# Six pairs of weight sums moved from the hidden loop to the gates' stage, in an fp32 encoder block on one core

## The reference

```python
h = rms(x, g_mix); z = h @ w_in
za, zu, zv, zq, zg = split(z)
ya = gelu(s5(za)); ya = (ya * sigmoid(ya @ w_glu + b_glu)) @ w_a_out
yb = sgu(zu, zv) @ w_b_out
yc = mem_xattn(zq, mem) @ w_c_out        # k, v from rms(mem, g_mem) @ w_kv
g = sigmoid(zg + b_gate)                 # three gates of width 1024
x = x + (g0 * ya + g1 * yb + g2 * yc) @ w_out
hf = rms(x, g_ffn)
x = x + (silu(hf @ w_gate) * (hf @ w_up)) @ w_down      # hidden width 2816
out = rms(x, g_final)
```

## Time and profile before

| what | value |
|---|---|
| median of three runs | 777.63 us |
| the profiled execution, its own time | 777.84 us |
| its span, first to last instruction | 776.1 us |
| TensorE busy | 765.6 us |
| VectorE busy | 541.6 us |
| ScalarE busy | 354.3 us |
| GpSimd busy | 315.8 us |
| DMA | 121.98 MB, 157 GB/s over the span |
| VectorE's sums (mix) | 44 operations, 47.2 us |

### The profile page before, as it was taken

The page is one execution under the profiler, slowest core; times in us unless marked ns, Lnnn a source line. Parts: engine busy times, 40 slices in busy tenths (PEclk is TensorE's granted clock), DMA queues, the critical chain, the costliest instruction groups (busy, mean ns, idle before and its releaser), DMA issues.

```text
span 776.1 us, 9751 instructions
## 1 busy us (share of the span) xinstructions
PE 765.6 (99%) x3576; PEld 630.8 (81%) x3576; DVE 541.6 (70%) x729; ACT 354.3 (46%) x526; POOL 315.8 (41%) x169
## 2 busy tenths in 40 slices
PE   9999999999999999999999999999999999999996
PEld 7778887788888888888888888888888888778885
DVE  6999997684848484345865677777776777635686
ACT  6896567644545434543433333332323233444463
POOL 4456646233333333444444344534444453920000
PEclk9999999999999999999999999999999999999999
DMA  7744332132222432232324465666756557677852
GB/s 274 297 142 135 110 109 86 31 102 82 82 82 82 132 139 82 82 108 84 106 96 146 147 206 180 214 230 203 228 186 196 204 200 246 196 246 249 280 179 109
DMA packets 39667, 121.98 MB, mean 157 GB/s; under 512 B 4048, under 2 KB 4176, under 8 KB 37840
## 3 DMA queue, kind: packets, MB, share of 16 engines
q1 hardware_dynamic: 39488, 121.26, 47.1%
q10 hardware_dynamic: 144, 0.26, 0.1%
HBM read 104.99 MB, written 16.52 MB: 157 GB/s over the span
## 4 chain that ended last, share of the span: by engine, by line
PE 78%; DVE 13%; ACT 3%; issue 2%; DMA 2%; POOL 1%; SPq 0%; POOLq 0%; DVEq 0%; ACTq 0%
PE bank L1557 21%; PE bank L1558 21%; PE bank L1559 21%; PE bank L1926 4%; PE bank L1928 4%; PE bank L1927 4%; DVE pow_tmp L969 3%; DVE tab_tmp L969 1%; DVE s5p L969 1%; PE bank L1798 1%; DMA xT<-xt_dram 1%; DMA raw<-mix_dram 1%; DVE m_lo L974 1%; ACT prob L655 1%; DVE h_lo L974 0%
## 5 line engine op out<-in xcount | busy, mean ns | idle before, releaser
L500 POOL TENSOR_TENSOR w_lo<-raw,w_hi 128x1024 fp32r<-128x1024 f32 x90 | 219.1, 2434 | 298.1 <-ACT w_hi L561 298.1
L561 ACT ACTIVATE w_hi<-raw 128x1024 fp32r<-128x1024 f32 x112 | 118.6, 1060 | 309.1 <-PE bank L1559 302.3
L1557 PE MATMUL bank<-h_hi,w_hi 128*128 128x512 f32 x608 | 238.2, 392 | 0.5 <-DVE th L969 0.4
L1559 PE MATMUL bank<-h_hi,w_lo 128*128 128x512 f32 x608 | 236.7, 389 | 0.0
L1558 PE MATMUL bank<-h_lo,w_hi 128*128 128x512 f32 x608 | 236.6, 389 | 0.0
L1557 PEld LDWEIGHTS bank<-h_hi,w_hi 128*128 128x128 f32 x608 | 114.1, 188 | 25.5 <-DVE th L969 1.3
L1559 PEld LDWEIGHTS bank<-h_hi,w_lo 128*128 128x128 f32 x608 | 114.1, 188 | 23.9
L1558 PEld LDWEIGHTS bank<-h_lo,w_hi 128*128 128x128 f32 x608 | 114.2, 188 | 23.3 <-issue 0.2
L505 POOL TENSOR_TENSOR w_lo<-raw,w_hi 128x512 fp32r<-128x512 f32 x48 | 67.2, 1422 | 56.3 <-ACT w_hi L561 49.7
L969 DVE TENSOR_TENSOR mix<-mix 128x512 f32<-128x512 f32 x44 | 47.2, 1072 | 10.5 <-DMA mix<-w_dram 9.4
L969 DVE TENSOR_TENSOR lo<-raw,hi 128x1536 fp32r<-128x1536 f32 (+1 forms) x19 | 33.3, 1757 | 28.8 <-ACT hi L888 28.8
(11 more groups left out here) (297 smaller groups left out, 1391.7 us busy)
## 6 DMA issues: line engine op xcount, KB each, us to landing
raw<-w_dram SPq DMA_DIRECT2D x112, 512.0 KB, 3.4
mix<-w_dram SPq DMA_DIRECT2D x11, 1024.0 KB, 7.7
mix_dram<-mix SPq DMA_DIRECT2D x11, 1024.0 KB, 6.4
raw<-w_dram SPq DMA_DIRECT2D x32, 256.0 KB, 3.9
raw<-mix_dram SPq DMA_DIRECT2D x28, 256.0 KB, 3.9
half_dram<-odd SPq DMA_DIRECT2D x11, 256.0 KB, 7.9
second<-half_dram SPq DMA_DIRECT2D x3, 768.0 KB, 6.0
raw<-mix_dram SPq DMA_DIRECT2D x3, 768.0 KB, 4.3
```

The source lines that it names most:

```text
L500: nc.gpsimd.tensor_tensor(w_lo[:, s, :], raw[:, s, :], fv(w_hi[:, s, :]), ALU.subtract).then_inc(w_ready, 1)
L561: nc.scalar.activation(w_hi[:, slot, :], raw[:, slot, :], ACT.Copy).then_inc(w_rounded, 1)
L1557: mm(out, a[0], b[0], start=first, stop=False)
L1559: return mm(out, a[1], b[0], start=False, stop=last)
```

## The change

It sets AHEAD = 6. The first six pairs are loaded, summed and stored in the stage T_J2 through three buffers: mix, mix_b (where uc was) and mix_c (where u was). SP issues these loads and stores between the weight tiles (`mix_ahead`), VectorE forms the sums between the gates (`mixed_ahead`). In the hidden loop turns 0 to 4 handle pairs 6 to 10, and turns 5 to 10 have no sums. The units get seven raw places, with a third raw_d and raw_e in the upper half of mix, and their loads another order. Three smaller edits: on VectorE the memory's `token_scale` moves ahead of the first S5 products; on ScalarE `round_weights(T_VU + 6)` moves ahead of `softmax_scale(2)`; on TensorE gate 0 of T_J1 waits for three sgu_taken, and the fourth is waited for before gate 1 of the first round.

```diff
@@ -54,6 +54,7 @@
 NS = 2
+AHEAD = 6
@@ -129,9 +130,10 @@
         raw_c = at("raw_c", o_s + (4 * C_BRE + 63) // 64 * 64, [P, TILE])
-        raw_d = [at(f"raw_d{i}", o_h + 12288 + 4096 * i, [P, TILE]) for i in range(2)]
-        unit_raw = [raw[:, 0, :], raw[:, 1, :], raw_c[:, :], raw_d[0][:, :], raw_d[1][:, :]]
-        UNIT_SLOT = (0, 1, 2, 3, 4, 0, 1, 2, 0, 1, 2)
+        raw_d = [at(f"raw_d{i}", o_h + 12288 + 4096 * i, [P, TILE]) for i in range(3)]
+        raw_e = at("raw_e", o_e + 12288, [P, TILE])
+        unit_raw = [raw[:, 0, :], raw[:, 1, :], raw_c[:, :], *(r[:, :] for r in raw_d), raw_e[:, :]]
+        UNIT_SLOT = (0, 1, 2, 3, 4, 5, 6, 0, 1, 2, 6)
         UNIT_DVE = (6, 8)
@@ -196,6 +198,7 @@
         mix = at("mix", o_e + 8192, [P, 4, WB])
+        mix_ring = [mix, at("mix_b", o_uc, [P, 4, WB]), at("mix_c", o_u, [P, 4, WB])]
         zg = at("zg", o_e, [P, 4, T])
@@ -282,7 +285,8 @@
         mix_loaded, mixed, mix_stored, half_stored = sems("mix_loaded mixed mix_stored half_stored")
-        unit_loaded = [sem(f"unit_loaded{i}") for i in range(5)]
+        unit_loaded = [sem(f"unit_loaded{i}") for i in range(7)]
+        ring_loaded = [mix_loaded, xtok_loaded[0], xtok_loaded[1]]
         unit_half, unit_dve, p5_done, s1_ready, s5_ready = sems("unit_half unit_dve p5_done s1_ready s5_ready")
@@ -382,37 +386,57 @@
             sp.dma_start(sgu[:, :, :], sgu_d).then_inc(sgu_loaded, 16)
+            def load_mix(n, buf, done=mix_loaded):
+                t = T_DN + 2 * n
+                sp.dma_start(buf[:, :, :].rearrange("p (a b) n -> p a (b n)", a=2),
+                             w_d[t:t + 2, :, :].rearrange("a p n -> p a n")).then_inc(done, 16)
+            def keep_mix(n, buf):
+                sp.wait_ge(mixed, 4 * (n + 1))
+                sp.dma_start(mix_d[n, :, :], buf[:, :, :].rearrange("p a n -> p (a n)")).then_inc(mix_stored, 16)
+            def mix_ahead(t):
+                n, odd_tile = divmod(t - T_J2 - 2, 2)
+                if odd_tile or n < 0:
+                    return
+                if n < AHEAD:
+                    if n == 0:
+                        sp.wait_ge(st_ready, ROUNDS)
+                    elif n < 3:
+                        sp.wait_ge(y_done, ROUNDS)
+                    else:
+                        sp.wait_ge(mix_stored, 16 * (n - 2))
+                    load_mix(n, mix_ring[n % 3], ring_loaded[n % 3])
+                if 2 <= n < AHEAD + 2:
+                    keep_mix(n - 2, mix_ring[(n - 2) % 3])
             for t in range(8, T_WO):
                 next_weights(t)
+                mix_ahead(t)
                 if t == T_J2 - 2:
...
                         load_x(i)
-            def load_pair(i):
-                t = T_DN + 2 * i
-                sp.dma_start(mix[:, :, :].rearrange("p (a b) n -> p a (b n)", a=2),
-                             w_d[t:t + 2, :, :].rearrange("a p n -> p a n")).then_inc(mix_loaded, 16)
-            def store_mix(i):
-                sp.wait_ge(mixed, 4 * (i + 1))
-                sp.dma_start(mix_d[i, :, :], mix[:, :, :].rearrange("p a n -> p (a n)")).then_inc(mix_stored, 16)
             def store_half(i):
...
                 next_weights(t)
+                mix_ahead(t)
                 i, j = divmod(t - T_FF, 4)
...
                     sp.wait_ge(x1_ready, 5)
-                    load_pair(0)
-                if i > 0 and j == 2:
-                    store_mix(i - 1)
+                    sp.wait_ge(mix_stored, 16 * AHEAD)
+                    load_mix(AHEAD, mix)
+                if 0 < i <= PAIRS - AHEAD and j == 2:
+                    keep_mix(AHEAD + i - 1, mix)
+                if 0 < i < PAIRS - AHEAD and j == 3:
+                    sp.wait_ge(mix_stored, 16 * (AHEAD + i))
+                    load_mix(AHEAD + i, mix)
                 if i > 0 and j == 3:
-                    sp.wait_ge(mix_stored, 16 * i)
-                    load_pair(i)
                     store_half(i - 1)
@@ -426,10 +450,12 @@
                     sp.wait_ge(w_ready, T_DN - 1 + k)
-                elif 3 <= k < 5:
+                elif 3 <= k < 6:
                     sp.wait_ge(w_used, T_DN)
-                elif k >= 5:
-                    unit_split(sp, {5: 0, 6: 1, 7: 2, 8: 5, 9: 6, 10: 7}[k])
+                elif k == 6:
+                    sp.wait_ge(mix_stored, 16 * PAIRS)
+                elif k > 6:
+                    unit_split(sp, {7: 0, 8: 1, 9: 2, 10: 6}[k])
                 sp.wait_ge(mix_stored, 16 * (k + 1))
@@ -460,14 +486,12 @@
                 load_unit(k)
-            store_mix(PAIRS - 1)
             for k in range(3, 6):
...
             store_half(PAIRS - 1)
-            for k in range(6, 10):
+            for k in range(6, PAIRS):
                 load_unit(k)
             load_three(0)
-            load_unit(10)
             load_three(1)
@@ -691,9 +715,9 @@
             round_weights(T_VU + 5)
+            round_weights(T_VU + 6)
             softmax_scale(2)
             gelu_u(1)
-            round_weights(T_VU + 6)
             round_weights(T_VU + 7)
@@ -882,7 +906,7 @@
                 if u == 0:
-                    act.wait_ge(w_ready, T_DN + 5)
+                    act.wait_ge(w_ready, T_DN + 6)
                 if u >= 2:
@@ -1097,6 +1121,8 @@
+            token_scale(2, 2, mtstd[:, :], mtrstd[:, :], mdiag[:, :, :], diag_m)
             bre, bim, cre, cim = (grid(c0) for c0 in (C_BRE, C_BIM, C_CRE, C_CIM))
@@ -1109,8 +1135,6 @@
             link(tt(bpow[1][:, L - 1, :, :], bb_tmp[:, 2, :, :], bb_tmp[:, 3, :, :], ALU.add))
-            token_scale(2, 2, mtstd[:, :], mtrstd[:, :], mdiag[:, :, :], diag_m)
             def times(to, of, a_re, a_im, conj, n):
@@ -1364,13 +1388,29 @@
+            def mix_sums(buf, count):
+                b11, b12, b21, b22 = (buf[:, j, :] for j in range(4))
+                tt(b22, b22, b12, ALU.subtract).then_inc(mixed, 1)
+                dve.wait_ge(mixed, count + 1)
+                tt(b12, b12, b11, ALU.subtract).then_inc(mixed, 1)
+                dve.wait_ge(mixed, count + 2)
+                tt(b11, b22, b11, ALU.add).then_inc(mixed, 1)
+                dve.wait_ge(mixed, count + 3)
+                tt(b21, b21, b11, ALU.subtract).then_inc(mixed, 1)
+            def mixed_ahead(n):
+                dve.wait_ge(ring_loaded[n % 3], 16 * (n // 3 + (1 if n % 3 == 0 else 2)))
+                mix_sums(mix_ring[n % 3], 4 * n)
             scale_gate0(0)
             scale_gate0(1)
+            mixed_ahead(0)
             for c in range(KB):
...
             scale_gate0(3)
+            mixed_ahead(1)
             for t in range(2):
@@ -1383,6 +1423,8 @@
             dve.wait_ge(y2_lo_s, KB)
+            mixed_ahead(2)
+            mixed_ahead(3)
             for g in (0, 2, 4, 6):
@@ -1392,7 +1434,11 @@
                     scale_gate0(g + 4)
+                    if g == 2:
+                        mixed_ahead(4)
                     scale_gate0(g + 5)
+                    if g == 2:
+                        mixed_ahead(5)
@@ -1418,21 +1464,16 @@
             a22, a12 = odd[:, 0:HALF], odd[:, HALF:T]
-            b11, b12, b21, b22 = (mix[:, j, :] for j in range(4))
-            with nc.vector.Fori(0, PAIRS) as i:
+            def hidden_pair(i, sums):
                 for n in range(2):
...
-                dve.wait_ge(mix_loaded, 16 * i + 16)
-                tt(b22, b22, b12, ALU.subtract).then_inc(mixed, 1)
-                dve.wait_ge(mixed, 4 * i + 1)
-                tt(b12, b12, b11, ALU.subtract).then_inc(mixed, 1)
-                dve.wait_ge(mixed, 4 * i + 2)
-                tt(b11, b22, b11, ALU.add).then_inc(mixed, 1)
-                dve.wait_ge(mixed, 4 * i + 3)
-                tt(b21, b21, b11, ALU.subtract).then_inc(mixed, 1)
+                if sums:
+                    dve.wait_ge(mix_loaded, 16 * i + 16 * ((AHEAD + 2) // 3 + 1))
+                    mix_sums(mix, 4 * i + 4 * AHEAD)
                 for n, hidden in enumerate((even, odd[:, :])):
@@ -1454,6 +1495,11 @@
                    ).then_inc(ff_lo, 1)
+            with nc.vector.Fori(0, PAIRS - AHEAD) as i:
+                hidden_pair(i, True)
+            with nc.vector.Fori(PAIRS - AHEAD, PAIRS) as i:
+                hidden_pair(i, False)
@@ -1757,7 +1803,7 @@
-            pe.wait_ge(sgu_taken, 4)
+            pe.wait_ge(sgu_taken, 3)
             pe.wait_ge(pt_act, 4)
@@ -1805,6 +1851,8 @@
                         pe.wait_ge(j1_g, free)
+                    elif b == 1:
+                        pe.wait_ge(sgu_taken, 4)
                     tile_ready(t0 + j)
```

## The result

The changed kernel took 784.16 us (median of four runs, 783.30 to 784.99), the kernel before beside it 777.62 (777.53 to 778.03). The ratio is 1.0082, 95% interval 1.0071 to 1.0094: slower by 6.5 us. I had forecast slower, but by 2, and the range ended at 782.0. The profiled execution took 784.99 us, with a span of 783.3.

The account below looks back on a forecast made before the run. TensorE's queue of matmuls sets the end, with at most some 10 us to win; -0.5 + 2.7 - 0.6 + 1.8 - 1.5 = +1.9 gave 779.7 against 777.84, 779.5 against the median. Range 775.2 to 782.0.

Parts of the forecast that it names:

- (1): Memory's row scale moves ahead of the tables on VectorE, removing TensorE's 0.42 us wait at 47.38: -0.5 us.
- (2): ScalarE rounds tile T_VU+6 ahead of the softmax scaling; holds by GpSimd make vM late for values(0): +2.7 us.
- rival D: Late tiles from traffic of (4), or a lower clock after TensorE's long stop: +1 to +3 on the forecast, chance 0.10.
- (3): Gate matmul waits for three sgu_taken, not four, removing the 0.43 us idle at 142.59: -0.6 us.
- (4): Six pairs' sums move from the hidden loop to the gates' stage; the last two groups delay merge0(4): +1.8 us.
- (5): Seven raw places in the down projection remove TensorE's waits before units 9 and 10: -1.5 us.

Follow-up runs that it names:

- e1: The changed kernel with the rounding of tile T_VU+6 put back behind softmax_scale(2) and gelu_u(1), nothing else; 778.46 us, ratio to before 1.0003.
- e4: As e1, with AHEAD = 4, so groups 4 and 5 are summed in the hidden loop again; 775.53 us, ratio to before 0.9971.
- e2: The changed kernel with 14 products of no use ahead of TensorE's wait for vM; 779.91 us, ratio to before 1.0024.
- e3: The kernel before with only the rounding of tile T_VU+6 moved ahead of softmax_scale(2); 781.39 us, ratio to before 1.0046.
- e7: As e1, with AHEAD = 2, so only groups 0 and 1 stay in the gates' stage; 775.05 us, ratio to before 0.9961.
- e5: As e1, but SP issues a group's store behind the odd tile, not right behind the load; 777.43 us, ratio to before 0.9993.
- e10: As e7, with the five raw places for units of before and their order of loads; 776.77 us, ratio to before 0.9988.
- e6: As e1, with the 24 sums in the gates' stage replaced by 24 small memsets, all loads and stores kept; 776.31 us, executions 774.69 to 778.07.
- e8: As e7, with the rounding of T_VU+6 between softmax_scale(2) and gelu_u(1), and vM ahead of the table sums; 777.12 us, ratio to before 0.9992.
- e9: As e8, with vM between head 3's last maximum and its snm, and head 3's reciprocal between the table sums; 773.80 us, ratio to before 0.9950.

## Why the prediction was wrong

Its steps, one by one, against the lateness in the traces:

| part | predicted | measured in the changed kernel | in other runs |
|---|---|---|---|
| (1) row scale | -0.5 | wait gone, 0 net at 118.85 | -0.4 to -0.5 (e1, e4) |
| (2) wait for vM | +2.7 | +2.5 | +2.5 (e2, e3) |
| (2) clock behind it | 0 (rival D: +2.3) | +3.0 | +1.8 (e3), 0 (e2) |
| (3) three sgu_taken | -0.6 | -0.7 | -0.7 (e1, e7); e3 has it without the edit |
| (4) gates' stage | +1.8 | +4.1 | +3.8 (e1), +2.3 (e2, e5), +0.6 (four groups), 0 (two) |
| (5) seven places | -1.5 | -1.8 | -1.8 (e1, e7), +0.5 with five (e10) |

**What held.** The chain of holds in (2) came out step by step: snm released at 128.67 for 128.8 predicted, vM at 132.25 for 132.4, values(0) at 132.30 for 132.5. That included its weakest link, that GpSimd would reach T_J1 0.2 us ahead of snm; it was 0.33. The prediction names only operations with two operands in SBUF as held, but snm has one (128x2, with a constant), and it took 2.09 us where the first snm took 0.17. In (4) without late tiles the trace of e5 also follows the working: merge0(4) 1.1 late for 1.3 predicted, a first wait of 0.40 in T_WO for 0.4, and 1.32 for mg_lo, where 379.8 to 381.7 less that 0.4 left 1.5. The waits are 1.72 of the 2.3; the rest are slow first products behind them, which I had left out. (5) was short by the slow products behind its two stops. (1) holds in e1 and e4: the lateness falls by 0.58 at the row scale, and 0.2 of it goes again at 61.94. In the changed kernel's profile ScalarE stood 1.00 us for memf at 28.70, and a wait of 0.40 for a w_lo at 36.19 took the gain back. e1 has the same list there and no such wait, so I count it to the execution.

**What failed** is one decision, twice: the two costs of rival D were left at nothing in the sum and given a chance of 0.10, as alternatives of each other. Both came, and both in the same run. The forecast of 779.5 with 3.0 for the clock and 1.8 for late tiles (4.1 less the 2.3 of e2 and e5) is 784.3; measured 784.16. That they agree to 0.1 is in part luck. Against the trace's +7.15 this sum is +6.7: (1) gave 0.5 less than I said and (4) without late tiles cost 0.5 more, (2), (3) and (5) together came out 0.6 better; and the medians lie 6.5 apart, not 7.15.

The first is the clock. I forecast a stop of 3.9 us, nine times the 0.43 of the earlier trace rows, and priced the products behind it at full speed since "no row here has the lower level". A missing row bounds nothing: the cost had two ends, 0 and half of some microseconds' work, and belonged into the sum. The Trainium skill, page "TensorE: Matmul & The Clock Gate", section "What's actually happening", says that idle time returns the engine to half rate. The windows agree: from 1.00 to 0.50 during the stop here, 0.2 us behind its end in e3, and no fall in e2, whose one edit kept TensorE at work. The size was off as well: I priced ten products, but all that TensorE did in 5.8 us ran at half speed (132.3 to 138.1), 2.9 us lost.

The second is the step "A tile's load may be some 5 us late before its rounding is; I cost it at nothing". A stretch of 25 us of the stage moved 285 GB/s in the changed kernel (106 in before). A tile behind a load and a store of 1 MB took 9.2 us, 5.8 more than the usual 3.4 and 1.8 more than it had. I had the rate, 290, but used it as a mean, where the two megabytes are issued together just ahead of the next tile. The lateness is small (merge0(0) was 1.2 late), but a list with eight sums in it makes merge0(4) 3.4 us later than in e5 (4.5 against 1.1), since the last sum then falls behind one more subtraction of 2.4 us. For TensorE that is 1.8 us, for in e5 the same subtraction holds an mf instead. This link is read from the rows of four profiles with six groups (late tiles and two holds in the changed kernel and e1, neither in e2 and e5); no run delays a tile and changes nothing else, so it is argued, not proven.

One thing of the prediction was judged too well: (3) and the stop in (2) aren't independent. e3 shows that a late TensorE finds the fourth sgu_taken done in any case, so in the changed kernel (3) gave nothing that the delay hadn't given already.

The Trainium skill, page "SBUF — State Buffer", section "Who interferes with whom", says that the later of the two engines fully blocks. A held operation again ended soon behind the release, not its whole 0.69 later: the mf operation that e5's row at 370.51 shows (2.33 us) ended at 372.84, 0.55 behind the end of GpSimd's row (369.89 to 372.29). By the rule's full length (2) would have come to +3.3; measured +2.5. The measurement decides.

Still open: why tiles are late in some traces and not in others with the same list in this stage (e1 against e2), and the slower executions of e6.

## What to carry to other kernels

Work that fills the idle time of an engine off the critical path must fit together with its holds and with the lateness of its inputs. Two groups with slack behind them cost nothing (e7), two in front of an operation that TensorE waits for cost 3.2 us (the stage loses 3.8 in e1, 0.6 in e4). Where a change makes the critical engine stand for microseconds, add the clock to its price. And when an operation is held, look for another in the list that isn't and put it there. With a milder form of the reordering this turned a loss into a gain: counted from 47 us and against e7, TensorE comes to gate 0 with a delay of 2.2 us in e8 and 1.1 us early in e9.

## What the runs showed of the hardware

After a stop of 3.36 us the granted clock was at 0.50 until about 138.1, 5.8 us after TensorE had begun again; after one of 3.41 us (e3) it rose at 136.0, 3.7 us after. Fourteen products in the stop kept it at 1.00. Stops of 0.93 and 1.67 us, 6 us apart (e8), left the mean clock of the span at 0.999. The same four products took 1.72 us at the upper level and 3.58 at the lower.

A 0.5 MB tile landed 3.1 to 5.0 us after its issue between 300 and 380 us in before, which moved 106 GB/s from 320 to 345. In the changed kernel it took up to 9.2 us, with 1 MB transfers ahead of it and 285 GB/s from 325 to 350. With the same list of transfers it was at most 7.2 in e2.
